# RWKV core on one core: crossed evictions and one scaling go to ScalarE, straight evictions and three products to VectorE, chain parts move inside the rounds

## The reference, cut to what matters

```python
w_log = -softplus(-(w0 + tanh(mix(1) @ w1) @ w2)) - 0.5
decay = exp(-exp(w_log))                       # = exp(-exp(-0.5) * sigmoid(w0 + ...))
iclr  = sigmoid(a0 + (mix(4) @ a1) @ a2)
kk    = heads(k * k_k); kk = kk / max(norm(kk), 1e-12)
k_h   = heads(k * (1.0 + (iclr - 1.0) * k_a))
b_h   = kk * iclr
# per token: sa = S @ -kk;  S = S * w + sa b^T + v k^T;  o = S @ r
o     = groupnorm(o) ; o = (o + sum(r_h * k_h * r_k) * v_h) * g
```

## Time and profile before

| | us |
|---|---|
| median of 3 runs (lowest to highest) | 3632.11 (3629.02 to 3633.79) |
| the profiled execution, its own time | 3627.32 |
| its span in the trace | 3625.5 |
| PE busy | 3442.5 (95%) |
| DVE busy | 1941.2 (54%) |
| ACT busy | 1395.1 (38%) |
| POOL busy | 418.8 (12%) |

### The profile page before, as it was taken

How to read it: one execution, slowest core, us unless ns; L and a number is a source line. 1 busy time by engine, 2 the same in 40 slices (tenths; PEclk the granted TensorE clock), 3 DMA queues, 4 the chain that set the end, 5 groups by cost and what they waited for, 6 DMA issues and landing times.

```text
span 3625.5 us, 95343 instructions
## 1 busy us (share of the span) xinstructions
PE 3442.5 (95%) x40925; PEld 3228.3 (89%) x40925; DVE 1941.2 (54%) x3021; ACT 1395.1 (38%) x2344; POOL 418.8 (12%) x570
## 2 busy tenths in 40 slices
PE   7988899999999989999999999999899788999999
PEld 6977679999999855699999999999899666799999
DVE  7557755555346644365543446553374776465532
ACT  4535533443222533344432224442244454244421
POOL 0022221111000000011100101110000222211100
PEclk9999989999999999999999999999999999999999
DMA  3210002222222387422222222222222000122222
GB/s 121 93 38 5 4 26 93 81 85 85 87 87 80 121 305 297 171 84 81 81 90 88 88 82 84 81 86 88 88 76 88 10 4 27 40 85 86 81 90 85
DMA packets 97093, 314.74 MB, mean 87 GB/s; under 512 B 19074, under 2 KB 20354, under 8 KB 96018
## 3 DMA queue, kind: packets, MB, share of 16 engines
q1 hardware_dynamic: 88706, 288.79, 23.7%
q10 hardware_dynamic: 8080, 21.34, 1.6%
HBM read 297.30 MB, written 12.79 MB: 86 GB/s over the span
## 4 chain that ended last, share of the span: by engine, by line
PE 88%; DVE 7%; ACT 3%; issue 2%; DMA 0%; SPq 0%; DVEq 0%; ACTq 0%
PE ps L418 24%; PE ps L416 23%; PE ps L417 23%; PE ps L1462 4%; PE ps L1017 1%; PE ps L2045 1%; DVE m L1507 1%; PE ps L2144 1%; PE ps L1646 1%; PE ps L2080 1%; PE ps L1128 1%; PE ps L2100 1%; PE ps L1138 1%; DVE arb L1495 1%; PE ps L2052 1%
## 5 line engine op out<-in xcount | busy, mean ns | idle before, releaser
L416 PE MATMUL ps<-xh,wh 128*128 128x288 f32 x4656 | 1386.0, 298 | 3.0 <-DVE xl L2430 1.9
L418 PE MATMUL ps<-xh,wl 128*128 128x288 f32 x4656 | 1381.5, 297 | 0.0
L417 PE MATMUL ps<-xl,wh 128*128 128x288 f32 x4656 | 1358.7, 292 | 0.0
L391 ACT ACTIVATE wh<-raw 128x1024 fp32r<-128x1024 f32 x415 | 440.2, 1061 | 1247.5 <-PE ps L418 1209.4
L417 PEld LDWEIGHTS ps<-xl,wh 128*128 128x128 f32 x4656 | 888.9, 191 | 1.7 <-issue 0.5
L416 PEld LDWEIGHTS ps<-xh,wh 128*128 128x128 f32 x4656 | 876.1, 188 | 7.5 <-issue 3.5
L418 PEld LDWEIGHTS ps<-xh,wl 128*128 128x128 f32 x4656 | 873.6, 188 | 0.0
L398 DVE TENSOR_TENSOR wl<-raw,wh 128x1024 fp32r<-128x1024 f32 x415 | 508.4, 1225 | 519.7 <-ACT wh L391 513.8
L418 PE MATMUL ps<-hh,wl 128*128 128x288 f32 x1536 | 457.7, 298 | 0.0
L416 PE MATMUL ps<-hh,wh 128*128 128x288 f32 x1536 | 453.9, 295 | 0.0
L417 PE MATMUL ps<-hl,wh 128*128 128x288 f32 x1536 | 453.9, 295 | 0.0
(11 more groups left out here) (360 smaller groups left out, 4927.1 us busy)
## 6 DMA issues: line engine op xcount, KB each, us to landing
raw<-in_w SPq DMA_DIRECT2D x415, 512.0 KB, 3.5
kp<-in_cache_k SPq DMA_DIRECT2D x64, 512.0 KB, 5.5
vp<-in_cache_v SPq DMA_DIRECT2D x64, 512.0 KB, 5.8
rkv<-in_wkv ACTq DMA_DIRECT2D x2, 2048.0 KB, 9.7
out_wkvs<-rkv ACTq DMA_DIRECT2D x2, 2048.0 KB, 7.2
out_k<-qk ACTq DMA_DIRECT2D x1, 2304.0 KB, 8.2
out_v<-vg ACTq DMA_DIRECT2D x1, 2304.0 KB, 14.0
out_x<-x SPq DMA_DIRECT2D x8, 288.0 KB, 3.4
```

The lines of the kernel that those rows point to most:

```text
L391: act.activation(wh[:, c % SPL], raw[:, c % RAWS], ACT.Copy).then_inc(s_hi, 1)
L416: pe.matmul(out, w_h, rhs_h, start=(first and k == 0), stop=False)
L417: pe.matmul(out, w_h, rhs_l, start=False, stop=False)
L418: mm = pe.matmul(out, w_l, rhs_h, start=False, stop=(last and k == nk - 1))
```

## The change: what it does

1. The crossed evictions `d2t` and `d4t` go from DVE (two copies of 64 partitions) to ACT (two copies of 64 partitions). The evictions `d2` and `d4` go from ACT to DVE, one copy of 128 partitions each.
2. The scaling of `zz0` goes from DVE to ACT, behind the tanh of `zz1` in piece 4. The scaling of `zz1` is gone; its factor 0.5 is put into the bias of the first exponential, into constants of `kh` and of L1225, and into `bb`.
3. `bb` goes from POOL to DVE (piece 10), and so do `bst` and `kst` (piece 12).
4. PE issues each step in two halves of two chunks. A chain part of an even place still stands before the step, one of an odd place now stands between the halves. On ACT, DVE and POOL the evictions of a step come behind both places.

```diff
@@ prep_dve
             if k == 4:
-                dve.wait_ge(a_zz, B.cnt(2, 1))
-                dve.tensor_scalar(zz0, zz0, 0.5, 0.5, ALU.mult, ALU.add).then_inc(a_sg, 1)
                 after(dve, a_ex, B.cnt(3, 0))
-                dve.wait_ge(a_sg, B.cnt(2, 1))
+                dve.wait_ge(a_sg, B.cnt(1, 1))
                 dve.tensor_tensor_scan(flat(csum[:, 0]), ...
             if k == 6:
                 dve.wait_ge(a_zz, B.cnt(2, 2))
-                dve.tensor_scalar(zz1, zz1, 0.5, 0.5, ALU.mult, ALU.add).then_inc(a_sg, 1)
                 dve.wait_ge(a_cm, B.cnt(1, 1))
-                dve.wait_ge(a_sg, B.cnt(2, 2))
...
-                dve.scalar_tensor_tensor(kh[:, 0], t3, 1.0, row, ALU.add, ALU.mult).then_inc(a_kh, 1)
+                dve.scalar_tensor_tensor(kh[:, 0], t3, 2.0, row, ALU.add, ALU.mult).then_inc(a_kh, 1)
             if k == 10:
...
+                dve.wait_ge(a_kk, B.cnt(1, 1))
+                dve.scalar_tensor_tensor(bb, zz1, 1.0, kraw[:, 0], ALU.add, ALU.mult).then_inc(a_bb, 1)
+            if k == 12:
+                dve.wait_ge(a_bb, B.cnt(1, 1))
+                dve.wait_ge(a_ex, B.cnt(3, 1))
+                dve.tensor_tensor(sl["bst"][:], bb, pinv[:, 0], ALU.mult).then_inc(a_bk, 1)
+                dve.tensor_tensor(sl["kst"][:], kh[:, 0], pinv[:, 0], ALU.mult).then_inc(a_bk, 1)
             if k == 13:
                 dve.wait_ge(a_bo, B.cnt(1, 1))
-                dve.tensor_tensor(B.row(rkv, KD), z, B.row(rkv, 2 * KD), ALU.mult).then_inc(a_bon, 1)
+                dve.scalar_tensor_tensor(B.row(rkv, KD), z, 0.5, B.row(rkv, 2 * KD), ALU.mult, ALU.mult).then_inc(a_bon, 1)
@@ prep_act
                 half_tanh(act, B, zz1, KD).then_inc(a_zz, 1)
+                act.wait_ge(a_zz, B.cnt(2, 1))
+                act.activation(zz0, zz0, ACT.Identity, scale=0.5, bias=halves).then_inc(a_sg, 1)
             if k == 8:
...
-                act.activation(pinv[:, 0], csum[:, 0], ACT.Exp, scale=DECAY).then_inc(a_ex, 1)
+                act.activation(pinv[:, 0], csum[:, 0], ACT.Exp, scale=DECAY, bias=lnhalf).then_inc(a_ex, 1)
@@ prep_pool
-            if k == 10:
-                after(pool, a_kk, B.cnt(1, 1))
-                pool.tensor_tensor(bb, kraw[:, 0], zz1, ALU.mult).then_inc(a_bb, 1)
-            if k == 12:
...
-                pool.tensor_tensor(sl["bst"][:], bb, pinv[:, 0], ALU.mult).then_inc(a_bk, 1)
...
-                pool.tensor_tensor(sl["kst"][:], kh[:, 0], pinv[:, 0], ALU.mult).then_inc(a_bk, 1)
@@ INV
-            d2=("m2", "m1", 0, "copy", "", "m3", ("lt", "ktok")),
+            d2=("m2", "m1", 0, "move", "", "m3", ("lt", "ktok")),
-            d4=("m4", "m3", 2, "copy", "", "m1", ("d2", "d2t")),
+            d4=("m4", "m3", 2, "move", "", "m1", ("d2", "d2t")),
@@ inv_pe
-            for p in range(4 * part, 4 * part + 4):
+            for p in range(4 * part + 2 * behind, 4 * part + 2 * behind + 2):
...
-            mm.then_inc(a_m, 1)
+            if behind:
+                mm.then_inc(a_m, 1)
@@ inv_act
+                if how == "cross":
+                    for r, cross in zip(HEADS, HEADS[::-1]):
+                        op = act.activation(sl[to][r, of], half_of(bk, part)[cross], ACT.Copy)
@@ inv_dve
+                if how == "move":
+                    dve.tensor_copy(sl[to][:, of], half_of(bk, part)).then_inc(a_d, 1)
@@ half
                     for behind in range(2):
-                        if behind:
-                            inv_step(eng, inv, k, part)
                         for q, pos in enumerate(CHAIN_AT if chain else ()):
                             if pos == 2 * (2 * k + part) + behind:
                                 chain_part(eng, chain, q // 3, q % 3)
+                        inv_step(eng, inv, k, part, behind)
```

More of the change, by code:

```diff
@@ L7 @@
 from contextlib import ExitStack
+import math
 import numpy as np
@@ L143, in build_program @@
         qg8, gneps, eps, warm, root5 = small[:, 0:1], small[:, 1:2], small[:, 2:3], small[:, 3:4], small[:, 8:13]
+        halves, lnhalf = small[:, 4:5], small[:, 5:6]
         big = m.at
@@ L1305, in prep_pool @@
                 pool.tensor_tensor(pprev[:, 0], csum[:, 0], zz0, ALU.subtract).then_inc(a_cm, 1)
-            if k == 10:
-                after(pool, a_kk, B.cnt(1, 1))
-                pool.tensor_tensor(bb, kraw[:, 0], zz1, ALU.mult).then_inc(a_bb, 1)
-            if k == 12:
-                after(pool, a_bb, B.cnt(1, 1))
-                after(pool, a_ex, B.cnt(3, 1))
-                pool.tensor_tensor(sl["bst"][:], bb, pinv[:, 0], ALU.mult).then_inc(a_bk, 1)
-                after(pool, a_kh, B.cnt(2, 2))
-                pool.tensor_tensor(sl["kst"][:], kh[:, 0], pinv[:, 0], ALU.mult).then_inc(a_bk, 1)
         INV = dict(
@@ L1372, in copies_of @@
             return [(name, part) for r in rounds_of(prompt) for part in range(2) for name in r
-                    if steps_of(prompt)[name][3] == "copy"]
+                    if steps_of(prompt)[name][3] in ("copy", "cross")]
         def others_of(prompt):
@@ L1379, in others_of @@
                 for part in range(2):
-                    out += [(name, part) for name in r if steps_of(prompt)[name][3] != "copy"]
+                    out += [(name, part) for name in r if steps_of(prompt)[name][3] not in ("copy", "cross")]
                     if "lt" in r and prompt:
@@ L1434, in first_none, with inv_pe @@
             pass
-        def inv_pe(pe, B, k, part):
+        def inv_pe(pe, B, k, part, behind):
             inv, names = steps_of(B.prompt), rounds_of(B.prompt)[k]
-            for name in names:
+            for name in names if not behind else ():
                 if name == "lt":
@@ L1466, in inv_pe, with inv_act @@
                     mm = l_pe(pe, Bat(B.j, B.c + 1), p)
-            mm.then_inc(a_m, 1)
+            if behind:
+                mm.then_inc(a_m, 1)
         def half_of(bk, part):
             return bank(bk + part, 256).rearrange("p (c t) -> p c t", t=CT)
-        def inv_act(act, B, k, part):
+        def inv_act(act, B, k, part, behind):
+            if not behind:
+                return
             sl, inv, of = slots[B.s], steps_of(B.prompt), slice(4 * part, 4 * part + 4)
@@ L1476, in inv_act, with inv_dve @@
                 _, _, bk, how, _, to, _ = inv[name]
[L1477 to L1483, removed]
+                if how not in ("copy", "cross"):
+                    continue
+                act.wait_ge(a_m, B.own("m", 2 * k + part + 1))
+                if how == "cross":
+                    for r, cross in zip(HEADS, HEADS[::-1]):
+                        op = act.activation(sl[to][r, of], half_of(bk, part)[cross], ACT.Copy)
+                else:
+                    op = act.activation(sl[to][:, of], half_of(bk, part), ACT.Copy)
+                op.then_inc(a_e, 1)
+        def inv_dve(dve, B, k, part, behind):
+            if not behind:
+                return
             sl, inv, names = slots[B.s], steps_of(B.prompt), rounds_of(B.prompt)[k]
@@ L1501, in inv_dve @@
                 _, _, bk, how, by, to, _ = inv[name]
-                if how == "copy":
+                if how in ("copy", "cross"):
                     continue
+                if name == "d4":
+                    dve.wait_ge(a_p1, B.own("p", 1))
                 dve.wait_ge(a_m, B.own("m", 2 * k + part + 1))
[L1505 to L1508, removed]
+                if how == "move":
+                    dve.tensor_copy(sl[to][:, of], half_of(bk, part)).then_inc(a_d, 1)
                 elif how == "add":
@@ L1518, in inv_dve, with inv_pool @@
                 l_dve(dve, Bat(B.j, B.c + 1), part)
-        def inv_pool(pool, B, k, part):
+        def inv_pool(pool, B, k, part, behind):
+            if not behind:
+                return
             sl = slots[B.s]
@@ L1526, in inv_pool @@
             if k == 1 and part == 1 and B.prompt:
-                after(pool, a_d, B.own("d", others_of(True).index(("d2t", 1)) + 1))
+                after(pool, a_e, B.own("e", copies_of(True).index(("d2t", 1)) + 1))
                 pool.tensor_tensor(plus[:], sl["m4"][:], mview("ist").unsqueeze(1).to_broadcast([P, NCK, CT]),
@@ L2537, in _ @@
             dve.memset(gneps[:], GN_EPS)
+            dve.memset(halves, 0.5)
+            dve.memset(lnhalf, math.log(0.5))
             dve.memset(eps[:], RMS_EPS)
```

## The result

| | median us (lowest to highest) | against before |
|---|---|---|
| before | 3631.49 (3629.02 to 3633.79) | |
| the changed kernel | 3667.13 (3663.23 to 3667.57) | 1.0096 (95% interval 1.0078 to 1.0113) |

The change makes the kernel 35 us slower. The forecast was 3630, "no change", with 3650 as its upper end; the time lies beyond it.

A forecast was written before the change was run, and what follows sets the result against it. It took round trips of PE and evictions in the RWKV core windows (674 of 3625.5 us) as all the change could move; -0.2 us a full pass gave -2.2 us on 3632.1, so 3630 ("no change"), range 3602 to 3650.

The forecast's parts named there:

- Steps 3 to 7: ACT's eviction queue: crossed pairs and scaling make the chain's eviction about 1.5 us late, so step 7 begins +1.0 us late.
- the sum: All terms added: -0.2 us a full pass, -1.1 a layer, -2.2 us for two layers.
- 0.25 of it absorbed by PE's later work: Chain waits inside steps 7 and 8 overlap with the late start and absorb about 0.25 us: -0.25.
- Rival 3: ACT becomes the bound: its delay reaches PE whole, +1.0 to +1.2 us a pass, +16 us, 3648; chance 25%.
- Step 7 and the t3 chain: POOL's pprev and with it t3 come late, but PE's work up to step 9 covers that; uncovered, 0.4 us.
- Steps 9 to 12: With POOL empty there, rk on DVE falls from 1.57 to 0.68 us, releasing PE's bonus matmul earlier.
- the -0.7 of the sum: PE's gain at the bonus matmul from the faster rk: 0.65 us, rounded to -0.7 a pass.
- Steps 12 to 16: Three products more cost DVE 2.0 us; the second ark eviction moves from 302.48 to about 303.9 to 304.3.
- The -0.3 at step 16: Step 16's eviction comes at about 305.75 instead of 306.02, as a chain-eviction wait of 0.85 us goes: -0.3.
- The tail: From step 16, chain parts hold back second halves by +0.4 to +0.5 us, mostly covered by DVE's queue; net +0.05.
- The passes of the samples: Sample-preparing pass: +3.2 us at step 9 from eight-piece tanhs, -1.9 from faster L1220 and L1222, -0.5 behind: +0.8.

The follow-up runs named there:

- e7: The changed kernel plus three unused PE matmuls behind step 5 of every prompt pass but the first; 3641.06 us, ratio 1.0026 to the kernel before.
- e4: The changed kernel with odd chain parts put back behind the whole step on every engine; 3639.94 us, ratio 1.0022 to the kernel before.
- e6: The changed kernel reduced to the three products on DVE and the dropped scaling of zz1, all else as before; 3621.72 us, ratio 0.9970.
- e10: The kernel before with only bb moved to DVE and the scaling of zz1 dropped, bst and kst on POOL; 3621.20 us, ratio 0.9970.
- e3: The changed kernel with bst and kst back on POOL, bb staying on DVE; 3657.72 us, ratio 1.0068 to the kernel before.
- e5: The changed kernel with both the zz0 scaling and the crossed pairs back on DVE; 3628.93 us, ratio 0.9991 to the kernel before.
- e1: The changed kernel with the scaling of zz0 back on DVE before the scan; 3643.49 us, ratio 1.0028 to the kernel before.
- e2: The changed kernel with crossed pairs back on DVE and straight evictions on ACT; 3634.35 us, ratio 1.0004 to the kernel before.
- e9: The kernel before with the tanh of zz1 in sixteen 32-column pieces in every prompt pass but the first; 3664.10 us, ratio 1.0079.

## Why the prediction was wrong, step by step

The prediction followed one pass of the kernel before. Its places can be laid against the changed kernel's one full pass at 1.00, both counted in us from the start of step 3's eviction (287.03 before, 320.93 after):

| | before | changed | difference | forecast |
|---|---|---|---|---|
| scan begins | 2.83 | 3.90 | +1.07 | +1.1 |
| step 7 begins | 5.09 | 6.16 | +1.07 | +1.0 |
| `rk` begins | 11.95 | 12.73 | +0.78 | +0.75 |
| the bonus matmul of step 12 begins | 13.66 | 14.26 | +0.60 | +0.05 |
| second `ark` mask begins | 15.45 | 16.85 | +1.40 | +1.4 to +1.8 |
| step 16's eviction begins | 18.99 | 19.08 | +0.09 | -0.3 |
| step 17's eviction begins | 20.33 | 21.48 | +1.15 | near -0.25 |
| L1234 (now L1240) ends | 26.52 | 28.10 | +1.58 | near -0.2 |

It is one pass of each kernel, and single passes at the same clock differ by up to 2 us; the means are 31.35 us and, with the clock held (e7), 32.18.

**Steps 3 to 7.** The delay and its prices were right, as the first two rows show; a pair has 0.80 from start to start where 0.9 was taken, the scaling 0.71 where 0.62 was: it has a bias from memory, as the first exponential now has (L1295, 0.71 too). **The step that failed is the sum's use of this delay.** It was counted as time, +1.0 with 0.25 of it absorbed by PE's later work, at one speed. The sum has no term for PE's clock, so it put that at nothing. The rows show the clock halved behind the delay: +1.8 us in the mean of full passes, by e7, and 25 of the 35 us over the whole kernel. The forecast read "1.00" in the earlier trace rows and never asked what more idle time would do to it. Rival 3 named ACT as the bound and priced it at +1.0 to +1.2 a pass; without the clock that was near (0.8), with it (2.6) less than half, which is why even the range's end fell short. What e7 doesn't say is which idle time it takes: e4 is idle as long ahead of the scan and keeps its clock, so why the three parts had to come together is open.

**Step 7 and the t3 chain.** DVE waits 0.51 us for POOL's `pprev` (the forecast had this at nothing unless uncovered). The trace doesn't show what this alone costs.

**Steps 9 to 12.** Right in kind, too high in size. Timeline of PE before, then of DVE and POOL in the changed kernel, same passes:

```profile
300.69 1.10 PE L1138 MATMUL ps<-a_zz,con 128*128 128x512 f32 x2 [0.40 <-DVE a_zz L1217]
```

```profile
333.66 0.75 DVE L1216 SCALAR_TENSOR_TENSOR a_zz<-rkv,par,a_kn 128x512 f32<-128x512 f32 x1
...
340.01 0.42 DVE L1518 TENSOR_TENSOR m<-ps,m 128x256 f32<-128x256 f32 x1 [0.61 <-PE ps L1461]
...
342.41 0.42 DVE L1518 TENSOR_TENSOR m<-ps,m 128x256 f32<-128x256 f32 x1 [1.09 <-PE ps L1461]
...
347.22 1.27 POOL L1534 TENSOR_TENSOR m<-m,msk 128x512 f32<-128x512 f32 x1 [19.52 <-DVE m L1417]
347.41 1.62 DVE L1240 TENSOR_TENSOR ar<-rkv,p 128x512 f32<-128x512 f32 x1 [0.28 <-ACT p L1300]
```

`rk` fell from 1.57 to 0.75 (0.68 forecast) and all 16 do so. This is the -0.7 of the sum. But in the pass that the forecast followed PE had waited for it for 0.40 us only: the matmuls in front of L1138 start until 300.07 and end 0.22 later, where the forecast took PE as free at 300.05. A mean pass of e6, without the other parts, is 0.4 us shorter, just that. In the changed kernel `rk` ends at 334.41 and the bonus begins at 335.19: it no longer waits for `rk`, but PE itself comes 1.0 us later, so the 0.25 of cover that `rk` shows wasn't there for PE, and the table has +0.60 for a forecast of +0.05. e10 shows that POOL can keep `bst` and `kst`: it is enough that `bb`, whose run on POOL began before `rk`, goes.

**Steps 12 to 16.** The second `ark` mask begins at 337.78, right behind `kst` (337.18), 4.1 us behind the start of `rk`; before it was 3.5 (298.98 to 302.48), with 0.29 of that spent in a wait for PE. That is as forecast. `bst` and `kst` on DVE take 1.4 us of its time; by e10 against e6 they cost nothing in the end, by e3 some 10 us in the changed kernel. The -0.3 at step 16 didn't come (+0.09).

**The tail.** +0.05 was too low. The evictions of step 16 and step 17 (340.01, 342.41) lie 2.40 us apart, with a wait of 1.09 for PE; before, they lay 1.34 apart, and DVE had the second waiting for it. Between them stands the chain part inside step 17, in which PE makes a pause of 0.62 us before L1573 that the profile puts down to no wait. e5 against e6 prices all the places together at +8 us, 0.5 for each of 14 to 16 passes if it is spread evenly, where the forecast said -0.25 (-0.3 and +0.05).

The forecast also lacks L1240. Its median was 0.94 us before (L1234) and is 1.34 now, 1.62 in this pass, where it begins 0.19 behind POOL's addition to `m5` (L1534) and ends 0.54 behind the end of that addition. The runs take this apart: the median is 1.33 to 1.34 in all six kernels that have the chain parts inside the steps (the changed one, e1, e2, e3, e5, e7) and 0.92 to 0.98 in all eight that don't. So it comes with the places: L1240 mostly began 0.8 to 0.9 us behind the start of POOL's addition, and begins 0.5 or less behind it now, and the sooner it begins the longer it takes.

**The passes of the samples** were forecast at +0.8 and are +5.5 and +3.0 (38.07 and 37.02 us from scan to scan, 32.60 and 34.03 before; so 8.5 us of the span lie in two passes), at a clock of 0.87; in e7, with the clock mostly held, 34.8.

## What to carry to other kernels

In a stage of short matmuls that wait for evictions, PE's idle time can have a second price: here the 7 us behind it ran at 1.2 GHz. So before work is moved to the engine that evicts, ask not only whether the wait is covered but what the clock does if it isn't, and give that a term or a rival of its own; and test by giving PE useless matmuls in the gap. Read how long PE really waits in front of a place before a faster release of it is priced (0.40 us, not 0.65). Undo the parts of a change one by one and in pairs: three parts that cost 5 to 10 us each cost 46 together, and the one that paid (`bb` away from POOL with the dropped scaling, -11 us) was hidden under them.

## What was not expected of the hardware

- The cost isn't in proportion to the load: 1.05 us more on ACT per pass cost 1.5 us in all (interval -3 to +6), 2.3 us more cost 29.
- From 350 to 359 us, ahead of the fall, the longest wait of PE that the profile of the changed kernel names is 1.3 us (for the chain's state); PE was busy for 2.94 of 5.00 us. It was not one long gap; in e9 it was, of 2.68 us. In e4 PE was busy for 2.81 of the 5.00 us up to a scan, and the clock stayed at 1.00 for the 10 us behind it.
- A 512-column ACTIVATE whose bias is read from memory took 0.71 us (L1295), the same exponential without it 0.62 (L1287 before).
- Two ACTIVATEs that cross partitions do not overlap with each other or with the next: 0.77 us for two of 0.379.
